# Where a weight unit starts in its ring slot: the second down projection from column 24 in place of column 8

## The reference

```python
def conv_ffn(h, w_up, conv_w, conv_b, w_down):
    u = jnp.einsum("bsd,df->bsf", h, w_up)
    ...
    g, val = jnp.split(c, 2, axis=-1)
    return jnp.einsum("bsf,fd->bsd", jax.nn.gelu(g, approximate=True) * val, w_down)
...
        f = conv_ffn(h2, w_up[layer], conv_w[layer], conv_b[layer], w_down[layer])
        x = x + rms_norm(f, ffn_post_g[layer])
```

## The kernel before

| operand | past a multiple of 256 |
|---|---|
| ring slot, column 0 | 160 |
| ring slot, column 8 | 192 |
| ring slot, column 24 | 0 |
| `f_hi`, `f_lo`, `y_hi`, `y_lo`, side tiles | 192 |
| `a_hi`, `a_lo` | 64 |

## Time and profile before

### The profile page before, as it was taken

How to read it: one execution, slowest core, us unless ns; L and a number is a source line. 1 busy time by engine, 2 the same in 40 slices (tenths; PEclk the granted TensorE clock), 3 DMA queues, 4 the chain that set the end, 5 groups by cost and what they waited for, 6 DMA issues and landing times.

```text
span 758.9 us, 16885 instructions
## 1 busy us (share of the span) xinstructions
PE 749.4 (99%) x5994; PEld 728.1 (96%) x5994; DVE 581.2 (77%) x1071; ACT 447.7 (59%) x751; POOL 211.6 (28%) x138
## 2 busy tenths in 40 slices
PE   9999999999999999999999999999999999999997
PEld 8999999999999999999999989999999999988885
DVE  5898986768888877435977896799999999973333
ACT  6644455466665665445855666877666666643431
POOL 0477643460000000342563002522122122122220
PEclk9999999999999999999999999999999999999999
DMA  8565554555555567545443333455555555665651
GB/s 293 191 224 193 184 164 134 195 187 200 188 193 187 177 222 250 189 141 187 141 167 111 114 111 112 139 176 198 196 184 189 193 187 180 214 221 189 183 183 55
DMA packets 37919, 135.49 MB, mean 179 GB/s; under 512 B 4465, under 2 KB 4721, under 8 KB 37873
## 3 DMA queue, kind: packets, MB, share of 16 engines
q1 hardware_dynamic: 37728, 134.86, 53.3%
q10 hardware_dynamic: 144, 0.00, 0.0%
HBM read 133.80 MB, written 1.05 MB: 178 GB/s over the span
## 4 chain that ended last, share of the span: by engine, by line
PE 85%; DVE 5%; ACT 4%; issue 3%; POOL 2%; DMA 1%; DVEq 0%; SPq 0%; POOLq 0%; ACTq 0%
PE bank L1852 24%; PE bank L1853 23%; PE bank L1854 23%; PE bank L2295 4%; PE bank L2294 4%; PE bank L2293 4%; DVE w_lo L1168 2%; ACT w_hi L773 2%; POOL X L741 1%; DMA X<-in_x 1%; PE bank L1908 1%; PE bank L2125 1%; PE bank L2145 0%; ACT score L1063 0%; POOL w_lo L622 0%
## 5 line engine op out<-in xcount | busy, mean ns | idle before, releaser
L1852 PE MATMUL bank<-h_hi,w_hi 128*128 128x256 f32 x1372 | 386.1, 281 | 1.1 <-DVE h_lo L1180 1.0
L1853 PE MATMUL bank<-h_lo,w_hi 128*128 128x256 f32 x1372 | 383.0, 279 | 0.0
L1854 PE MATMUL bank<-h_hi,w_lo 128*128 128x256 f32 x1372 | 383.0, 279 | 0.0
L773 ACT ACTIVATE w_hi<-raw 128x1024 fp32r<-128x1024 f32 (+2 forms) x243 | 258.8, 1067 | 89.9 <-PE bank L2295 41.0
L1168 DVE TENSOR_TENSOR w_lo<-raw,w_hi 128x1024 fp32r<-128x1024 f32 (+2 forms) x187 | 236.1, 1264 | 94.3 <-ACT w_hi L773 92.3
L1852 PEld LDWEIGHTS bank<-h_hi,w_hi 128*128 128x128 f32 x1372 | 257.9, 188 | 2.7 <-DVE w_lo L1246 0.8
L1853 PEld LDWEIGHTS bank<-h_lo,w_hi 128*128 128x128 f32 x1372 | 257.9, 188 | 0.0
L1854 PEld LDWEIGHTS bank<-h_hi,w_lo 128*128 128x128 f32 x1372 | 257.8, 188 | 0.0
L622 POOL TENSOR_TENSOR w_lo<-raw,w_hi 128x1024 fp32r<-128x1024 f32 (+1 forms) x56 | 139.0, 2484 | 380.8 <-ACT w_hi L773 372.6
L1226 DVE TENSOR_TENSOR bank<-bank,scales 128x256 f32<-128x256 f32 x116 | 49.5, 430 | 26.2 <-PE bank L1854 17.6
L1507 DVE SCALAR_TENSOR_TENSOR cg<-bank,vec,cg 128x255 f32<-128x255 f32 x108 | 51.3, 475 | 0.7 <-ACT cg L1003 0.6
(11 more groups left out here) (232 smaller groups left out, 978.8 us busy)
## 6 DMA issues: line engine op xcount, KB each, us to landing
raw<-in_w_up SPq DMA_DIRECT2D x108, 512.0 KB, 3.3
raw<-in_w_in SPq DMA_DIRECT2D x53, 512.0 KB, 3.5
raw<-in_w_down SPq DMA_DIRECT2D x32, 512.0 KB, 4.1
raw<-in_w_down SPq DMA_DIRECT2D x16, 704.0 KB, 4.1
raw<-in_w_o SPq DMA_DIRECT2D x8, 512.0 KB, 3.3
raw<-in_w_gate SPq DMA_DIRECT2D x8, 512.0 KB, 3.4
raw<-in_w_out SPq DMA_DIRECT2D x8, 512.0 KB, 3.3
raw<-in_w_b_out SPq DMA_DIRECT2D x4, 512.0 KB, 3.7
```

What stands on the lines that cost most here:

```text
L773: nc.scalar.activation(hi_of(u)[:, cols], raw[s][:, cols], ACT.Copy).then_inc(hi_ready, 1)
L1852: nc.tensor.matmul(ps, wh, hi[:, k, :], start=start and n == 0, stop=False)
L1853: nc.tensor.matmul(ps, wh, lo[:, k, :], start=False, stop=False)
L1854: last = nc.tensor.matmul(ps, wl, hi[:, k, :], start=False, stop=stop and n == len(ks) - 1)
```

## The change

```diff
 def first_col(u):
 
-    return RING_PAST // 4 if u >= UNIT0["down2"] + LEAD else 0
+    return 3 * RING_PAST // 4 if u >= UNIT0["down2"] + LEAD else 0
```

## The result

The changed kernel takes 760.62 us in the median of 22 runs (759.97 to 763.15), the kernel before 759.97 us in as many (759.27 to 760.75). The ratio is 1.0013, 95% interval 1.0008 to 1.0019. So it is slower, by 0.65 us between the medians and by 1.0 us between the means (760.96 and 759.94 us): less than 0.2%, but clear of no change. The number hides what happened. The 22 runs are not one cloud: 17 lie between 759.97 and 760.92 us and five between 761.83 and 763.15 us. The first profile, at 761.95 us, belongs to the five.

The account below looks back on a forecast made before the run. The prediction took the matmul engine to bound the kernel. 348 matmuls x 0 ns, plus 0 for preparation and tail, left the 760.1 us median unchanged; range 757.7 to 762.5 us.

Parts of the forecast that it names:

- What bounds the kernel, and where the change is paid: Matmul engine bounds the span, busy 749.4 of 758.9 us; the change is paid in the second down projection's 348 matmuls.
- Preparation and tail cost nothing: Rounding and subtracting weights stay hidden, with 1.58 us cover per unit; work after the last matmul keeps its length: 0.
- I take no change in the step: Second down projection: start-to-start time of the 348 matmuls stays 226.7 ns; chance 0.53 for up to 4.4 ns either way.
- the nearest row: 256-column matmuls of `y` and `a` against the ring's weights differ by 2.0 ns, so at most 0.7 us either way.
- The explanation of the dear value: Column 0's 233.3 ns against column 8's 226.7 was laid to a moving operand not starting on 64 bytes.
- The faster rival: Distance between operand addresses sets the price on a rising line; 348 matmuls save up to 2.3 us, 757.8 us; chance 0.24.
- The slower rival: Operand distance repeats after 128 bytes, so each of 348 matmuls pays some 6.7 ns: +2.3 us, 762.4 us; chance 0.23.
- The rule of independent read ports: Skill rule: weight load and moving stream don't share read bandwidth, so the moving address alone would count, 0.7 us.
- the side tiles: With the same moving `y`, 256-column matmuls took 120.0 ns against these and 116.8 ns against the ring's weights.

Follow-up runs that it names:

- column 0 throughout: All units of the second down projection start at weight column 0, against the kernel before: median 762.13 us, ratio 1.0028.
- Column 40: The 29 later units start at weight column 40 instead of 8 of the kernel before, stationary minus moving +128 bytes: 762.12 us, ratio 1.0026.
- column 16 with moved tiles: Kernel before with the second down projection's stationary tiles laid 32 bytes further and the later units at weight column 16, distance 0: 760.27 us, ratio 1.0005.
- column 16: The 29 later units start at weight column 16 instead of 8 of the kernel before, stationary minus moving -32 bytes: 762.18 us, ratio 1.0027.
- column 72: The 29 later units start at weight column 72, 256 bytes past column 8 of the kernel before: 759.64 us against 759.85, ratio 1.0000.
- the added matmul: Changed kernel (column 24) with one more matmul at the start of the stage, its result overwritten by the next: one run, 762.54 us.
- the idle stretch: Changed kernel (column 24) with one more wait, for unit 6, before the stage's 37th matmul: four runs, 765.55, 765.77, 767.01 and 767.18 us.

## Why the prediction was wrong, by its own steps

*What bounds the kernel, and where the change is paid*: right. The stage is bound by the step of its 348 matmuls, a column's price shows there and nowhere else, and column 0 throughout turned a stage of 2.3 us more into runs 2.3 us longer. *Preparation and tail cost nothing*: right, no wait changed its order and the last start stays 5.9 us ahead of the end of the span. But the prediction misread as column 0 against column 8. The preparation runs ahead: ScalarE's three roundings from 667.58 us on are units 3 to 5, already in column 8, as are those after them.

```profile
667.58 1.05 ACT L773 ACTIVATE w_hi<-raw 128x1024 fp32r<-128x1024 f32 x1
...
672.88 1.04 ACT L773 ACTIVATE w_hi<-raw 128x1024 fp32r<-128x1024 f32 x1
674.58 1.06 ACT L773 ACTIVATE w_hi<-raw 128x1024 fp32r<-128x1024 f32 x1 [0.66 <-PE bank L2295]
```

With all units in column 0 the later roundings take the same 1.06 us, so no run shows the column moving the preparation at all:

```profile
L773 ACT ACTIVATE w_hi<-raw 128x1024 fp32r<-128x1024 f32 x25 | 26.6, 1062 | 42.3 <-PE bank L2295 42.3
```

*"I take no change in the step"*: this failed. It rested on the nearest row, a difference of 2.0 ns between two moving operands that both start on a multiple of 64 bytes. Those rows were 256-column matmuls against another stationary address. Their distances were -32 and +96, and none was -64. The step measured 2.2 ns more in some executions and 6.65 ns more in others. Since most runs of the first set had the short step, 0.8 us in all, the time still lies within 0.2%, and the median of 760.62 us lies inside the range; but it moved up beyond its interval, and no change was the forecast. That it came so near is luck: in the first set 17 of 22 runs had the lower time, in the second four of eight, with a median of 761.36 us. The 0.2% that the prediction took as the least that can be told from no change was also too coarse: the interval of 22 runs is 0.06% either way.

*The explanation of the dear value* ("the one moving operand that doesn't start on a multiple of 64 bytes") failed too. Column 40 is on 64 bytes and takes 233.3 ns; column 16 with moved tiles is off them and takes 226.7.

*The faster rival* had the right quantity and the wrong curve. Distance decides, but zero is the cheap point among 512-column matmuls, and both sides of it are dearer. I had drawn one line through rows of two shapes: with 256 columns -32 is cheaper than 0, with 512 columns column 16 at -32 costs 6.6 ns more than column 8 at 0.

*The slower rival* had the right size for the long step, 233.3 ns, and 762.4 us for runs with it, where the five stand at 761.83 to 763.15 us. Its reason, a period of 128 bytes, is wrong: column 40 shows that 128 doesn't bring the cheap step back, column 72 that 256 does. Its chance of 0.23 was given to the whole of the runs, whereas the step differs from execution to execution.

*What no rival had*: one program with two steps. The hint stood in the trace of before. Column 0 alternates between 232 and 235 ns, by twos, while the three products come by threes. So the stream seems to carry a state from one matmul to the next, and a new column is entered in one of two phases.

*The rule of independent read ports* (the Trainium skill, TensorE: Matmul & The Clock Gate, Part 2): column 16 speaks against it as the side tiles did in the prediction, since it went from 233.3 to 226.7 ns when the stationary tiles alone were laid elsewhere. That the two reads meet in some part of the memory would explain it, but no run shows that they do, or where.

## What to carry to other kernels

Where TensorE is the bound, read the start-to-start step of each shape by operand address before moving anything: here one matmul costs 226.7 to 233.3 ns by the distance of its two operands within 256 bytes, and distance 0 was the cheap one for 512 moving columns and not for 256. Take such a price only from rows of the same shape and the same distance. When the median moves by less than the trace explains, look at the single runs: two groups mean two behaviours of one program, and a profile shows only one of them.

## What the runs showed that was not expected

A distance of -64 bytes gives the same program two settled steps, 228.9 and 233.3 ns, kept through all 348 matmuls, and the phase of the alternation before the switch (235 or 232 ns in the last step) went with the choice in four profiles of four. Whether the phase is the cause is not shown, for the added matmul is one run and the idle stretch left the question open. What sets it in a run is not known; it was seen to differ between executions of one program. The first block's 256-column matmuls at -32 showed two steps as well, 116.7 and 117.8 ns, with nothing changed there. A distance of 0, on the other hand, was found from irregular beginnings: column 72 and the moved tiles took five and ten uneven steps and then held 226.7 ns.
